# RWKV projection of a hybrid decoder step: sums, bonus products and low-rank products in another order, and two stores awaited a stage later

## What is computed

```python
f = (u + mu * (prev - u)).astype(f32)
new_buf = u[:, -1]
r, k, v = f[..., :d], f[..., d:2 * d], f[..., 2 * d:3 * d]
w_lo, a_lo, g_lo = f[..., 3 * d:o1], f[..., o1:o2], f[..., o2:]
w_log = -jax.nn.softplus(-(w0 + jnp.tanh(w_lo) @ w_up)) - 0.5
a = jax.nn.sigmoid(a0 + a_lo @ a_up)
g = jax.nn.sigmoid(g_lo) @ g_up
kk = heads(k * k_k)
kk = kk / jnp.maximum(jnp.sqrt(jnp.sum(kk * kk, axis=-1, keepdims=True)), 1e-12)
k = k * (1.0 + (a - 1.0) * k_a)
bonus = jnp.sum(rh * kh * r_k, axis=-1, keepdims=True) * vh
```

## Time and profile before

| | us |
|---|---|
| median of 3 runs | 2954.49 (2952.33 to 2960.16) |
| profiled execution, span from first to last instruction | 2949.8 |
| median less that span | 4.7 |
| TensorE busy | 2693.6 (91%) |
| projection of layer 1, about | 1485 to 1632 |
| tiles of layer 1, about | 1632 to 1740 |

### The profile page before, as it was taken

How to read it: one execution, slowest core, us unless ns; L and a number is a source line. 1 busy time by engine, 2 the same in 40 slices (tenths; PEclk the granted TensorE clock), 3 DMA queues, 4 the chain that set the end, 5 groups by cost and what they waited for, 6 DMA issues and landing times. The chain is left out here.

```text
span 2949.8 us, 62087 instructions
## 1 busy us (share of the span) xinstructions
PE 2693.6 (91%) x24092; PEld 2462.7 (83%) x24092; DVE 1872.8 (63%) x3117; ACT 1352.8 (46%) x2294; POOL 841.2 (29%) x696
## 2 busy tenths in 40 slices
PE   7987889999999899899989878799999998998998
PEld 6876459999989689899978764599999895998998
DVE  4854457777766655489448454577777676554893
ACT  4733354545444244354357333555554442533542
POOL 0030009999910400000000300199999004000000
PEclk9999989999998999999989999899999998999999
DMA  5423459677545376365453243696866344764544
GB/s 134 110 59 105 138 100 148 117 129 122 83 79 161 97 202 168 104 166 139 126 115 101 65 132 112 115 141 115 139 106 104 74 141 124 199 172 108 161 133 120
DMA packets 838374, 365.86 MB, mean 124 GB/s; under 512 B 406189, under 2 KB 825558, under 8 KB 837512
## 3 DMA queue, kind: packets, MB, share of 16 engines
q1 hardware_dynamic: 835858, 360.77, 53.7%
q10 hardware_dynamic: 2232, 1.26, 0.2%
HBM read 342.63 MB, written 61.23 MB: 137 GB/s over the span
## 5 line engine op out<-in xcount | busy, mean ns | idle before, releaser
L1213 PE MATMUL key_banks<-w_kb_head,latent_T_head 128*128 128x352 f32 x1536 | 519.5, 338 | 9.7 <-DVE latent_T_rest L1341 9.7
L1213 PE MATMUL key_banks<-w_kb_head,latent_T_rest 128*128 128x352 f32 x1536 | 497.1, 324 | 0.0
L1213 PE MATMUL key_banks<-w_kb_rest,latent_T_head 128*128 128x352 f32 x1536 | 496.6, 323 | 0.0
L297 DVE TENSOR_TENSOR w_rests<-w_ring,w_heads 128x2048 fp32r<-128x2048 f32 (+1 forms) x150 | 321.6, 2147 | 146.9 <-ACT w_heads L291 146.7
L1355 DVE TENSOR_REDUCE w_kb<-key_sq 128x8 f32<-128x1024 f32 x256 | 311.2, 1216 | 12.4 <-ACT key_sq L1278 7.7
L1213 PEld LDWEIGHTS key_banks<-w_kb_head,latent_T_head 128*128 128x128 f32 x1536 | 290.5, 189 | 23.5 <-DVE latent_T_rest L1341 11.6
L1213 PEld LDWEIGHTS key_banks<-w_kb_rest,latent_T_head 128*128 128x128 f32 x1536 | 290.9, 189 | 0.0
L1213 PEld LDWEIGHTS key_banks<-w_kb_head,latent_T_rest 128*128 128x128 f32 x1536 | 289.8, 189 | 0.0
L291 ACT CAST w_heads<-w_ring 128x2048 fp32r<-128x2048 f32 (+1 forms) x150 | 268.4, 1792 | 42.8 <-ACT conv_last_rows L1934 19.7
L1033 POOL TENSOR_TENSOR rwkv_state_tmp<-rwkv_state,vec 128x1024 f32<-128x1024 f32 x64 | 153.3, 2395 | 455.6 <-POOLq L232 450.7
L1265 ACT CAST latent_T_head<-turn_bank 128x256 fp32r<-128x256 f32 x256 | 95.3, 372 | 400.6 <-PE key_banks L1217 392.2
(11 more groups left out here) (597 smaller groups left out, 7006.1 us busy)
## 6 DMA issues: line engine op xcount, KB each, us to landing
w_ring<-in_ffn_w_up_dram SPq DMA_DIRECT2D x88, 512.0 KB, 5.0
page_latents<-in_cache_kv_latent_dram SPq DMA_DIRECT2D x256, 128.0 KB, 2.4
latent_blocks<-page_latents SPq DMA_DIRECT2D x256, 128.0 KB, 3.9
latents<-page_latents SPq DMA_DIRECT2D x64, 512.0 KB, 8.4
w_ring<-in_w_in_dram SPq DMA_DIRECT2D x52, 512.0 KB, 3.8
w_ring<-in_w_gate_dram SPq DMA_DIRECT2D x46, 512.0 KB, 4.0
w_ring<-in_w_in_dram SPq DMA_DIRECT2D x20, 1024.0 KB, 5.9
w_ring<-in_ffn_w_down_dram SPq DMA_DIRECT2D x32, 384.0 KB, 3.3
```

Of the source, the lines that this page charges most:

```text
L297: ops.tensor_tensor(rests[:, slot, 0:tiles * P], ring[:, slot, 0:tiles * P], heads[:, slot, 0:tiles * P].bitcast(F32), ALU.subtract).then_ ...
L1213: last = nc.tensor.matmul(kbank[:, 3 * x + n, 0:KB], c[:, x, r * P:(r + 1) * P], w[:, r, cols], start=r == 0 and m == 0, stop=r == 1 and m ...
```

## The change

The low-rank products use half of the array's rows each: w reads rows 0 to 63, a rows 64 to 127, from one shared `lo` without zeros, and the two memsets that made the zeros go. They are spread over units 2, 3 and 4 (three, three and two tiles), with three banks each for w and a. kk's sums follow one unit later on PE (tile d behind unit d+4), and with them the gate products (d+5) and ACT's gate copies (d+6); both take other banks. DVE's `rk` is split: the bonus product moves one or two units ahead, the multiply by the decay stays where it was and is now `rho`. SP no longer waits for the two stores of the last rows; the semaphore lives across the stages, and DVE waits for it in the tiles ahead of `BR`, the first buffer there that lies over the stored rows and is written. The tiles' stage clears it.

```diff
-    LORA = {2: range(0, 4), 3: range(4, 8)}
+    LORA = {2: range(0, 3), 3: range(3, 6), 4: range(6, 8)}
+    W_BANK, A_BANK, KK_BANK, G_BANK = (2, 3, 6), (4, 5, 7), (6, 7), (4, 5)
-    SQUARE, CLAMP, GATE = 3, 4, 4
+    SQUARE, CLAMP, GATE = 3, 4, 5
-    RK = {13: 0, 15: 1, 20: 2, 23: 3}
+    RK = {12: 0, 14: 1, 18: 2, 21: 3}
+    RHO = {13: 0, 15: 1, 20: 2, 23: 3}
...
-        lo = pairs[:, 0, :, :]
+        lo = pairs[:, 0, 0, :]
...
-        turned, rows_out, stored = st.sem("last_transposed"), st.sem("last_rows_ready"), st.sem("last_stored")
+        turned, rows_out, stored = st.sem("last_transposed"), st.sem("last_rows_ready"), k.shift_stored
...
-                sp.wait_ge(stored, 32)
...
-                    if d >= 2:
-                        pe.wait_ge(w_sig, d - 1)
-                        pe.wait_ge(a_sig, d - 1)
-                    nc.tensor.matmul(banks[:, 2 + d % 2, 0:T], wa_up[:, cols], lo[:, 0, :], start=True, stop=True).then_inc(w_made, 1)
-                    nc.tensor.matmul(banks[:, 4 + d % 2, 0:T], wa_up[:, cols], lo[:, 1, :], start=True, stop=True).then_inc(a_made, 1)
+                    if d >= 3:
+                        pe.wait_ge(w_sig, d - 2)
+                        pe.wait_ge(a_sig, d - 2)
+                    nc.tensor.matmul(banks[:, W_BANK[d % 3], 0:T], wa_up[0:64, cols], lo[0:64, :], start=True, stop=True).then_inc(w_made, 1)
+                    nc.tensor.matmul(banks[:, A_BANK[d % 3], 0:T], wa_up[64:128, cols], lo[64:128, :], start=True, stop=True).then_inc(a_made, 1)
...
                     if d == 0:
-                        pe.wait_ge(w_sig, DT)
-                        pe.wait_ge(a_sig, DT)
+                        pe.wait_ge(w_sig, 6)
+                        pe.wait_ge(a_sig, 6)
...
                         pe.wait_ge(lo_ready, 3)
+                        pe.wait_ge(w_sig, DT)
+                        pe.wait_ge(a_sig, DT)
...
-                    if SQUARE <= s < SQUARE + DT:
-                        kk_length(s - SQUARE)
+                    if SQUARE < s <= SQUARE + DT:
+                        kk_length(s - SQUARE - 1)
...
                     last.then_inc(rk_ready, 1)
+
+                def rho(p):
                     dve.wait_ge(rk_ready, p + 1)
...
-                nc.vector.memset(lo[64:128, 0, :], 0.0).then_inc(lo_zero, 1)
-                nc.vector.memset(lo[0:64, 1, :], 0.0).then_inc(lo_zero, 1)
...
+                    if s in RHO:
+                        rho(RHO[s])
...
+        st.adopt([k.shift_stored])
...
                     keep("l", g, L, g)
+                dve.wait_ge(k.shift_stored, 32)
...
+            k.shift_stored = nc.alloc_semaphore("shift_rows_stored")
```

More of the change, by code:

```diff
@@ L2147, in rwkv_enter @@
             "mix_rows_loaded", "param_rows_loaded", "state_rows_loaded", "shift_rows_loaded", "broadcast_rows_loaded", "lora_weights_loaded"))
[L2148 to L2149 removed]
+        p_turned, p_copied, s_turned, s_copied, kept_ready = (st.sem(n) for n in (
+            "param_rows_turned", "params_copied", "state_rows_turned", "states_copied", "complements_ready"))
         squared, summed, inverse, scaled, headed, rested = (st.sem(n) for n in (
             "squared", "squares_summed", "inverse_root_ready", "norm_scaled", "norm_headed", "norm_rested"))
[L2152 removed]
+        turned, rows_out, stored = st.sem("last_transposed"), st.sem("last_rows_ready"), k.shift_stored
         lo_ready, w_made, a_made, g_made, w_sig, a_sig, g_kept = (st.sem(n) for n in (
@@ L2242, in kk_length @@
                     if d == 0:
-                        pe.wait_ge(w_sig, DT)
-                        pe.wait_ge(a_sig, DT)
+                        pe.wait_ge(w_sig, 6)
+                        pe.wait_ge(a_sig, 6)
                     elif d >= 2:
                         pe.wait_ge(kk_cut, d - 1)
-                    nc.tensor.matmul(banks[:, 2 + 2 * (d % 2), 0:T], k.col("block64"), squares[:, d % 2, :], start=True, stop=True).then_inc(kk_sum, 1)
+                    nc.tensor.matmul(banks[:, KK_BANK[d % 2], 0:T], k.col("block64"), squares[:, d % 2, :], start=True, stop=True).then_inc(kk_sum, 1)
                 def lora_g(d):
@@ L2252, in lora_g @@
                         pe.wait_ge(lo_ready, 3)
+                        pe.wait_ge(w_sig, DT)
+                        pe.wait_ge(a_sig, DT)
                     elif d >= 2:
                         pe.wait_ge(g_kept, d - 1)
-                    nc.tensor.matmul(banks[:, 3 + 2 * (d % 2), 0:T], g_up[:, d * P:(d + 1) * P], k.fT[:, 25, :], start=True, stop=True).then_inc(g_made, 1)
+                    nc.tensor.matmul(banks[:, G_BANK[d % 2], 0:T], g_up[:, d * P:(d + 1) * P], k.fT[:, 25, :], start=True, stop=True).then_inc(g_made, 1)
                 def bonus(p):
@@ L2343, in sigmoids @@
                     act.wait_ge(w_made, d + 1)
-                    nc.scalar.activation(k.alphaT[:, d, :], banks[:, 2 + d % 2, 0:SEQ], ACT.Sigmoid, bias=k.par("rwkv_w0", d))
-                    nc.scalar.activation(k.samT[:, 1, d, :], banks[:, 2 + d % 2, SEQ:T], ACT.Sigmoid, bias=k.par("rwkv_w0", d)).then_inc(w_sig, 1)
+                    nc.scalar.activation(k.alphaT[:, d, :], banks[:, W_BANK[d % 3], 0:SEQ], ACT.Sigmoid, bias=k.par("rwkv_w0", d))
+                    nc.scalar.activation(k.samT[:, 1, d, :], banks[:, W_BANK[d % 3], SEQ:T], ACT.Sigmoid, bias=k.par("rwkv_w0", d)).then_inc(w_sig, 1)
                     act.wait_ge(a_made, d + 1)
-                    nc.scalar.activation(k.aT[:, d, :], banks[:, 4 + d % 2, 0:T], ACT.Sigmoid, bias=k.par("rwkv_a0", d)).then_inc(a_sig, 1)
+                    nc.scalar.activation(k.aT[:, d, :], banks[:, A_BANK[d % 3], 0:T], ACT.Sigmoid, bias=k.par("rwkv_a0", d)).then_inc(a_sig, 1)
                 def square(d):
@@ L2412, in _ @@
                         act.wait_ge(mixed, 1)
-                        act.wait_ge(lo_zero, 2)
-                        nc.scalar.activation(lo[0:64, 0, :], k.fT[0:64, 24, :], ACT.Tanh).then_inc(lo_ready, 1)
-                        nc.scalar.copy(lo[64:128, 1, :], k.fT[64:128, 24, :]).then_inc(lo_ready, 1)
+                        nc.scalar.activation(lo[0:64, :], k.fT[0:64, 24, :], ACT.Tanh).then_inc(lo_ready, 1)
+                        nc.scalar.copy(lo[64:128, :], k.fT[64:128, 24, :]).then_inc(lo_ready, 1)
                     if s == 2:
```

8 lines of the change are left out of this document (2 added, 6 removed).

## The result

The changed kernel took 2926.16 us (median of 4 runs, 2921.26 to 2929.01) where the kernel before took 2954.03 (4 runs, 2952.33 to 2960.16): ratio 0.9905, 95% interval 0.9883 to 0.9926. A second set of runs gave 0.9911 (0.9898 to 0.9923). It is faster, as forecast, but by 27.9 us where 16.6 was forecast, and 2926.16 lies under the range, which ended at 2929.0.

What follows compares the result with a forecast made beforehand. TensorE was taken to bound the projection's first part, then ACT, then DVE. A lead of 5.4 plus 2.9 for stores made 8.3 per layer, 16.6 for both: 2937.9 us, range 2929 to 2947.

Steps and rivals of the forecast that it cites:

- Low-rank products, -3.4: Projection, w and a products: row halves run side by side, saving 3.87 a layer less 0.5 for entering and leaving.
- The rivals of no or partial overlap: Low-rank row halves: no overlap, total 2945.7, chance 0.08; overlap only in part, total 2939.3, chance 0.13.
- the 77%: Low-rank products: at 77% of the possible, 2.71 instead of 3.87 a layer would go, total an estimated 2940.2.
- Lead of 5.3 at ACT's stretch: TensorE reaches the stretch where ACT is full earlier by 3.4 + 0.7 + 0.3 + 0.9 us a layer.
- ACT's stretch, +0.6 and -0.7: Where ACT is full: later gate copies cost 0.6, the bonus wait behind unit 16 saves 0.7; lead becomes 5.4.
- my own rule: For all TensorE waits: a wait is worth its length only if the engine waited for isn't full.
- the other three: Bonus waits other than that behind unit 16, 3.4 us: should return as waits for `mix`, counted 0.
- DVE's stretch, 0: Where DVE is 98% busy: splitting `rk` changes only order, so nothing is gained and the 5.4 lead carries on.
- Stores, -2.9: Projection's end: SP's wait for its two stores goes whole, 2.9 us a layer.
- The clock kept into the tiles: Tiles' begin: TensorE stays at 2.4 GHz after less idle, 1.44 a layer more saved, total 2935.0; chance 0.20.
- The slower rival: Projection, 1553 to 1592: TensorE idles longer and falls to 1.2 GHz, total up to 2971.9; chance 0.08.

## Why the prediction was wrong

The direction and most of the terms held; two terms were too small, that of ACT's stretch and that of the stores, and the range ended too early below. The forecast 2937.9 missed 2926.2 by 11.7. Of that 4.9 lie between first unit and tiles, 1.6 ahead of the first units, 2.8 in the stages outside, and 2.4 in the distance from span to median, which I kept at 4.7 and which was 2.3.

- **Low-rank products, -3.4:** near, 3.0 when taken out, 2.8 by units. The rivals of no or partial overlap are refuted: the records start in pairs every 0.24. The Trainium skill ("TensorE: Matmul & The Clock Gate", Part 3) has a measured 3.07 for four row tiles; the 77% that I carried over to halves was an estimate. The trace shows all of the possible but the 0.2 that a visit spends entering and leaving (1.65, against six pairs of records at 0.24), and 0.1 more ahead of it (0.23 behind the unit's last record, where it is 0.13 before).
- **Lead of 5.3 at ACT's stretch:** right as a sum, 6.1 and 5.2, repeated at 5.1 and 5.1. Its parts hold only together: the halves' 3.4 gave nothing alone, and the later sums, for which I gave 1.9, are worth 4.7 of the lead when taken out of the whole, 1.6 of it in clock. That an early sum eats the halves' gain stands nowhere in the forecast; that the sum came out right owes something to luck.
- **ACT's stretch, +0.6 and -0.7:** the step that failed. The stretch gave 2.5 a layer where the sum had 0.1. Of the four bonus waits I priced one, the 0.68 behind unit 16, and let "the other three" come back as waits for `mix` in DVE's stretch. But one of these three, 1.40, stands behind unit 14, in ACT's stretch, and DVE, for which TensorE waits there, has 31.76 of 39 and isn't full; by my own rule that wait was worth its length. Below stand its row and, from the changed kernel, the waits ahead of units 16 and 17, the only ones of TensorE there from unit 8 to unit 17:

```profile
1581.56 1.24 PE L2266 MATMUL u_banks<-actor_then_bonus_product,const 128*128 128x288 f32 x4 [1.40 <-DVE actor_then_bonus_product L2510]
```

```profile
1559.00 0.37 PE L304 MATMUL u_banks<-h_heads_T,w_heads 128*128 128x288 f32 x1 [0.39 <-DVE fT L2470]
...
1564.66 0.37 PE L304 MATMUL u_banks<-h_heads_T,w_heads 128*128 128x288 f32 x1 [1.27 <-DVE fT L2470]
```

The wait that I left unpriced went for good, and in place of the one that I priced stands a longer one. In the runs the bonus products' move is worth 1.3 to 1.9 in this stretch for my 0.7. The sums' move is worth 0.6 to 1.2 there for my -0.6. Of that some 0.5 is the second clamp wait, behind unit 8, which takes 4.15 where it took 4.67. The squares themselves came nearer to what I had: with the sums' move alone units 9 and 10 give 3.3, and the units up to 17 take 3.0 back, 1.3 of it as longer waits for bonus products (2.42 behind unit 14).

- **DVE's stretch, 0:** right, -0.2, with the bonus waits back as waits for `mix` as forecast.
- **Stores, -2.9:** right in the projection, 2.84, and the new wait ahead of `BR` cost nothing. By the runs the term failed too: two times 2.9 make 5.8, and the stores alone gave 12.4 (8.0 to 16.6). I let nothing follow behind the tiles' begin; some 7 us do, at a higher granted clock, and their cause stays open.
- **The clock kept into the tiles:** not here; the changed kernel's first groups took 3.49 and 3.34, for 3.56 and 3.54.
- **The range** took the projection's bounds as the whole. It left out what the stages outside do: they vary by more than 10 from one execution to the next, and they too came out shorter with the wait moved.

The slower rival was refuted for this kernel (clock 1.00 in both full stretches), but its mechanism is real: it is what the kernel with early sums shows.

## What to carry to other kernels

Price every wait at its place: the list of waits gives only totals, and the timeline tells in which stretch each one stands and whether the engine waited for is full there. A wait for the full engine comes back elsewhere for the most part; one for an engine that only has its work in another order can go for good. Parts of a change that feed one another can't be priced one by one: halves that gave nothing alone gave 3.0 a layer once the sums behind them came later and a third bank was there. Where executions spread by 20 us, compare the stage in the profiles, from a place at which they repeat, and hold the runs against it: what the two disagree by is an effect somewhere else.

## What the runs showed of the hardware

A pause of 2.1 us in the middle of the projection dropped TensorE to its lower level for some 3 us (in both layers, by the length of unit 4), while pauses of 2.88 and 2.89 at one place of the program did so in one execution and not in another. Behind the 2.38 at the tiles' begin, the first 64x64 group ran at the higher level throughout in 2 of 18 cases (2.10 us), and in part in 3 (2.71 to 2.90); in the other 13 it took 3.32 to 3.69. Behind 5.2 of idle it took 3.42 to 3.69 in all 10 cases. An f32 product on 64 rows costs next to nothing beside one on the other 64: the two start within 0.01 us, and pairs of records follow every 0.24 us, where single records on the whole array follow every 0.23. GpSimd's two-operand multiplies slowed DVE's instructions beside them, the bonus product by 24%; its multiply and add with a scalar for each row left the projection faster.
